# The latents' norm behind the experts: once per layer over all 512 tokens, or tile by tile beside the next tile's expert places

## What is computed

```python
def _rmsnorm(x, w):
    y = xf * lax.rsqrt(jnp.mean(xf * xf, axis=-1, keepdims=True) + EPS)
    return (y * w).astype(x.dtype)
for l in range(DEPTH):                       # DEPTH = 2
    h = _rmsnorm(x, norm1[l]) * (1 + sc1) + sh1
    x = x + g1 * _token_mixer(h, ...)[0]
    h = _rmsnorm(x, norm2[l]) * (1 + sc2) + sh2
    x = x + g2 * _peer(h, ...)               # 8 heads x 16 picked experts for each token
y = _rmsnorm(x, final_norm)
```

## Time and profile before

| | us |
|---|---|
| median of three runs | 4971.81 |
| the profiled execution | 4934.85 |
| its span in the trace | 4933.1 |
| PE busy | 3932.0 (80%) |
| DVE busy | 3078.9 (62%) |
| POOL busy | 2831.9 (57%) |
| ACT busy | 1199.2 (24%) |

### The profile page before, as it was taken

The page is one execution under the profiler, slowest core; times in us unless marked ns, Lnnn a source line. Parts: engine busy times, 40 slices in busy tenths (PEclk is TensorE's granted clock), DMA queues, the critical chain, the costliest instruction groups (busy, mean ns, idle before and its releaser), DMA issues.

```text
span 4933.1 us, 40947 instructions
## 1 busy us (share of the span) xinstructions
PE 3932.0 (80%) x11544; PEld 1863.3 (38%) x11544; DVE 3078.9 (62%) x6951; ACT 1199.2 (24%) x2524; POOL 2831.9 (57%) x2642
## 2 busy tenths in 40 slices
PE   5798889889777777788776787999787777777776
PEld 3674444334333333344342454444332222222222
DVE  8637898775556556555655777852557566566653
ACT  2433333211223222232111343231112111111111
POOL 0001556317677677777766444630767777777775
PEclk8798889999999999999999898999999999999999
DMA  8653889758999999999988766962889999999997
GB/s 306 230 180 144 295 312 389 272 199 318 345 365 358 356 379 379 379 400 400 380 327 336 254 230 238 369 242 79 313 333 379 367 384 383 370 398 383 389 392 299
DMA packets 425891, 1585.40 MB, mean 321 GB/s; under 512 B 47680, under 2 KB 55360, under 8 KB 408640
## 3 DMA queue, kind: packets, MB, share of 16 engines
q0 software_dynamic: 376800, 1394.77, 74.8%
q1 hardware_dynamic: 44256, 183.81, 10.0%
q10 hardware_dynamic: 4608, 4.20, 0.3%
HBM read 1577.87 MB, written 4.72 MB: 321 GB/s over the span
## 4 chain that ended last, share of the span: by engine, by line
PE 20%; DMA 18%; issue 5%; POOL 3%; DVE 2%; ACT 1%; DVEq 1%; ACTq 0%; POOLq 0%
PE pair L744 19%; DMA vbuf_lat<-in_expert_v,idx_lat 17%; POOL ubuf_lat L709 2%; POOL vbuf_lat L716 1%; DVE acc L1747 0%; PE pair L880 0%; PE pair L885 0%; DMA ubuf_ctx<-in_expert_u,idx_ctx 0%; DVE ubuf_ctx L1698 0%; DMA ubuf_lat<-in_expert_u,idx_lat 0%; ACT L1128 0%; DVEq L1569 0%; DVE hist_lat L1566 0%; DVEq L1741 0%; ACT on_lat L1128 0%
## 5 line engine op out<-in xcount | busy, mean ns | idle before, releaser
L744 PE MATMUL pair<-vbuf_lat,diag 128*128 128x512 f32 x4096 | 2036.2, 629 | 706.6 <-DMA vbuf_lat<-in_expert_v,idx_lat 674.6
L744 PEld LDWEIGHTS pair<-vbuf_lat,diag 128*128 128x128 f32 x4096 | 731.8, 195 | 1946.4 <-DMA vbuf_lat<-in_expert_v,idx_lat 1042.3
L716 POOL DMA_INDIRECT vbuf_lat<-in_expert_v,idx_lat x1024 | 1133.9, 1107 | 464.8 <-issue 220.1
L1698 DVE CUSTOM_DVE_ANT_0 ubuf_lat<-hT,ubuf_lat 128x1024 f32<-128x1024 f32 x768 | 936.1, 1224 | 702.2 <-DMA ubuf_lat<-in_expert_u,idx_lat 698.1
L709 POOL DMA_INDIRECT ubuf_lat<-in_expert_u,idx_lat x1024 | 1089.9, 1064 | 376.8 <-issue 226.2
L744 PE MATMUL pair<-hT,slot 128*128 128x512 f32 (+1 forms) x2048 | 578.3, 442 | 24.4 <-DVE hT L1428 15.9
L1128 ACT ACTIVATE diag<-cst,coef 128x128 f32<-128x128 f32 x1024 | 326.6, 390 | 1004.4 <-DVE coef L1704 1000.4
L709 POOL DMA_INDIRECT ubuf_ctx<-in_expert_u,idx_ctx x256 | 292.3, 1142 | 482.7 <-DVE araw L1698 307.3
L1698 DVE CUSTOM_DVE_ANT_0 ubuf_lat<-xnat,ubuf_lat 128x1024 f32<-128x1024 f32 x256 | 312.0, 1224 | 250.4 <-DMA ubuf_lat<-in_expert_u,idx_lat 248.3
L744 PEld LDWEIGHTS pair<-hT,slot 128*128 128x128 f32 x2048 | 319.2, 196 | 275.4 <-issue 262.4
L1128 ACT ACT_TABLE_LOAD x318 | 408.0, 1283 | 31.9 <-DVE mT_lat L1592 15.2
(11 more groups left out here) (313 smaller groups left out, 3148.7 us busy)
## 6 DMA issues: line engine op xcount, KB each, us to landing
slot<-in_w_query SPq DMA_DIRECT2D x32, 1024.0 KB, 5.6
modw<-in_w_mod_turned POOLq DMA_DIRECT2D x28, 1024.0 KB, 5.7
slot<-in_w_qk SPq DMA_DIRECT2D x16, 1024.0 KB, 6.8
slot<-in_w_v SPq DMA_DIRECT2D x16, 1024.0 KB, 5.9
slot<-in_w_r SPq DMA_DIRECT2D x16, 1024.0 KB, 7.9
wraw<-in_w_zg SPq DMA_DIRECT2D x32, 512.0 KB, 6.5
wraw<-in_w_zf SPq DMA_DIRECT2D x32, 512.0 KB, 6.5
wraw<-in_w_gla_out SPq DMA_DIRECT2D x32, 512.0 KB, 6.5
```

The source lines that it names most:

```text
L716: pool.indirect_dma_start(peer[s].v[n % ring_v][:, :], None, v_rows, bass.IndirectOffsetOnAxis(ap=index[:, p // PICKS, p % PICKS:p % PICKS ...
L744: return pe.matmul(out, lhsT, rhs, start=first, stop=last)
L1698: v.tensor_tensor_reduce(rows_of, x, rows_of, 1.0, 0.0, ALU.mult, ALU.add, araw[n % 3][:, p % GS:p % GS + 1]).then_inc(s_dot, 1)
```

## The change

The norm behind the experts is made per tile of 128 tokens. A new piece `tile_norms(l)` is woven into the experts of layer l on PE, ACT and DVE; its due times follow `updated_us(t)`, the time planned for the end of the tile's second update. It uses a 128 x 128 tile `tile_rs` and the columns 0 to 127 of `ps[1]`. The squares, the sum of squares, `rstd` and `norm` go out of the head of `mix(1, LAT)`, and `last_norm(LAT)` goes. The outputs are laid out in HBM by tile, and `y_sample` is stored in four pieces of one tile each, as each is normed.

```diff
+def updated_us(t):
+    return lat_place(PICKS * (t + 1) + 27) + 0.5 if t < TS // P - 1 else lat_added(TS // P * PICKS // GS) + 6.5
...
+            # PE
+            def tile_norms(l):
+                for t in range(NT[LAT]):
+                    yield updated_us(t) + 3.0
+                    n = l * NT[LAT] + t
+                    pe.wait_ge(s_tsq, n + 1)
+                    need(pe, s_trs, n)
+                    pe.wait_ge(s_xnc, l * (NT[0] + NT[1]) + NT[0] + NT[1])
+                    c0 = TP + t * P
+                    for k in range(KC):
+                        last = mm(ps[1][:, 0:P], ones[:, :], hT[:, k, c0:c0 + P], k == 0, k == KC - 1)
+                    last.then_inc(s_tss, 1)
...
+            # ACT
+            def tile_norms(l):
+                for t in range(NT[LAT]):
+                    n, c0 = l * NT[LAT] + t, TP + t * P
+                    yield updated_us(t) + 1.5
+                    act.wait_ge(s_xu[LAT], 2 * (n + 1))
+                    af(hT[:, :, c0:c0 + P], xT[:, :, c0:c0 + P], ACT.Square).then_inc(s_tsq, 1)
+                    yield updated_us(t) + 5.0
+                    act.wait_ge(s_tss, n + 1)
+                    need(act, s_th, n)
+                    af(tile_rs[:, :], ps[1][:, 0:P], ACT.Ln, bias=eps[:, :], scale=1.0 / D)
+                    act.drain()
+                    af(tile_rs[:, :], tile_rs[:, :], ACT.Exp, scale=-0.5).then_inc(s_trs, 1)
...
+            # DVE
+            def tile_norms(l):
+                for t in range(NT[LAT]):
+                    n, c0 = l * NT[LAT] + t, TP + t * P
+                    yield updated_us(t) + 8.0
+                    dve.wait_ge(s_trs, n + 1)
+                    h = hT[:, :, c0:c0 + P]
+                    spread = lambda column: column.to_broadcast([P, KC, P])
+                    tt(h, xT[:, :, c0:c0 + P], tile_rs[:, :].unsqueeze(1).to_broadcast([P, KC, P]), ALU.mult)
+                    dve.drain()
+                    if l == DEPTH - 1:
+                        tt(h, h, spread(cols0[:, 16:24].unsqueeze(2)), ALU.mult).then_inc(s_th, 1)
+                        continue
+                    tt(h, h, spread(nscale[l + 1][:, 0, :, LAT:LAT + 1]), ALU.mult)
+                    dve.drain()
+                    tt(h, h, spread(modT[l + 1][:, 0:KC, LAT:LAT + 1]), ALU.add).then_inc(s_th, 1)
...
             # SP
-            for k in range(0, KC, 2):
-                hold(sp, s_h[LAT], 2 * DEPTH * KC + k + 2)
-                sp.dma_start(y_sample[:, k:k + 2, :], hT[:, k:k + 2, COLS[LAT]]).then_inc(s_y, 16)
+            for t in range(NT[LAT]):
+                hold(sp, s_th, (DEPTH - 1) * NT[LAT] + t + 1)
+                sp.dma_start(y_sample[t], hT[:, :, TP + t * P:TP + (t + 1) * P]).then_inc(s_y, 16)
```

More of the change, by code:

```diff
@@ L453, in build @@
     assert e[0] <= end, (e[0], end)
+    tile_rs = place("tile_rs", [P, P], at=[area[CTX].end - P * 4])
     CONTEXT_BANK, CONTEXT_TURN = (0, 4), (0, 3)
@@ L536, in build @@
         s_x2 = [sem(f"x_done_of{s}") for s in range(2)]
+        s_tsq, s_tss, s_trs, s_th = sem("tile_squares"), sem("tile_square_sums"), sem("tile_rstd"), sem("tile_normed")
         s_zero = sem("zeros_set")
@@ L570, in z_no, with norm2_no @@
             return (2 * l + s) * KC + z
+        def norm2_no(l, s):
+            return 2 * l + 1 if s == CTX else l + 1
         def unit_no(l, s):
@@ L778, in mix @@
                     pe.wait_ge(s_sc, 2 * (2 * l) * PH)
-                sum_squares(s, 2 * l, b.ss)
+                by_tiles = s == LAT and l > 0
+                if not by_tiles:
+                    sum_squares(s, 2 * l, b.ss)
                 yield at(-9.0)
@@ L782, in mix @@
                 for k in range(KC):
-                    pe.wait_ge(s_h[s], (2 * l) * KC + k + 1)
+                    if by_tiles:
+                        pe.wait_ge(s_th, l * NT[LAT])
+                    else:
+                        pe.wait_ge(s_h[s], (2 * l) * KC + k + 1)
                     last = mm(b.lr, a.wlr[:, k, :], hs[k], k == 0, k == KC - 1)
@@ L958, in mix @@
                 pe.wait_ge(s_x1[s], l * KC + KC)
-                sum_squares(s, 2 * l + 1, b.ss)
+                sum_squares(s, norm2_no(l, s), b.ss)
             def loaded_qk(l, s, h):
@@ L1156, in mix @@
                     squares(s, None)
-                else:
+                elif s == CTX:
                     squares(s, (2, (l - 1) * KC))
@@ L1163, in mix @@
                     states(0)
-                rstd(s, 2 * l, b.ss)
+                if s == CTX or l == 0:
+                    rstd(s, 2 * l, b.ss)
                 yield at(-6.0)
@@ L1269, in mix @@
                 yield at(NORM2_US + 7.0)
-                rstd(s, 2 * l + 1, b.ss)
+                rstd(s, norm2_no(l, s), b.ss)
             def natural(l, s, t, source, dst):
@@ L1489, in mix @@
                 yield at(-28.0)
-                norm(s, 2 * l, lambda k: nscale[l][:, 0, k, s:s + 1], lambda k: modT[l][:, k, s:s + 1])
+                if s == CTX or l == 0:
+                    norm(s, 2 * l, lambda k: nscale[l][:, 0, k, s:s + 1], lambda k: modT[l][:, k, s:s + 1])
                 dve.wait_ge(s_tab, 16)
@@ L1598, in mix @@
                 yield at(NORM2_US + 9.0)
-                norm(s, 2 * l + 1, lambda k: nscale[l][:, 1, k, s:s + 1], lambda k: modT[l][:, 24 + k, s:s + 1])
+                norm(s, norm2_no(l, s), lambda k: nscale[l][:, 1, k, s:s + 1], lambda k: modT[l][:, 24 + k, s:s + 1])
             def choose(l, s, u, at):
```

27 lines of the change are left out of this document (12 added, 15 removed).

## The result

| | before | after |
|---|---|---|
| median of 20 runs each, same chip | 4962.37 us | 4973.95 us (4954.72 to 4983.75) |
| ratio | | 1.0024, 95% interval [1.0013, 1.0036]: +12 us [6, 18] |
| profiled execution, span | 4934.85, 4933.1 us | 4969.39, 4967.6 us |

The changed kernel is a little slower: the interval leaves "no change" out, but the difference is less than the 0.3% that the prediction had set as the least that can be told, and the time is inside the forecast range. The two profiled executions differ by 34.5 us. Part of that is chance: single executions of one kernel lie 30 to 50 us apart, and the profiled one of before was faster than all its runs here. I compare short stretches that begin at the same event, over as many traces as have them.

A forecast was written before the change was run, and what follows sets the result against it. Bound: the gather stream, tied to PE, in layer 1's experts; a chain over the norm before the mixer. Terms -10.1 - 9.8 + 11.1 + 8.7 + 2.0 = +1.9 us on median 4971.81: 4973.7, range 4960 to 4988 (4950 to 4992 with rivals).

The forecast's parts named there:

- The tail, -9.8: Behind layer 1's last tile: the shorter norm chain and last store end the span at 4923.3, 9.8 us earlier.
- sum to 4914.35: In layer 1's last tile norm: PE's sum of squares over 128 columns takes 1.95 us, ending at 4914.35.
- The mixer, -10.1: Between layer 0's experts and the next mixer: the norm per tile saves 10.1 us, bounds 7 to 18.5.
- PE resumes 10.1 us earlier: Into layer 1's mixer: PE could start 18.5 us earlier, but waits for DVE's key copy, which moves 10.1 us earlier.
- the shift stays: Behind the key copy: the mixer keeps its order and is PE-bound, so the 10.1 us gain lasts.
- Six mid-tile norms, +19.8: Tiles 0 to 2 of each layer: a 4.3 us stall each, costing 11.1 us in layer 1 and 8.7 in layer 0.
- the tiles are no longer than before: Sign of being wrong: the six gaps appear, yet the tiles do not lengthen (3 to 4 us each expected in layer 1).
- DVE's wait is covered: Mid-tile: dots come some 9 us late, hidden behind the held v gather; if not, 2 to 4 us more each.
- The rival with +7 for each norm there: Layer 0: DVE's backlog makes each of three norms cost about 2.9 + 7 us; sum +23, 4995; chance 0.18.
- The six stalls are swallowed: Rival, mid-tile: gathers in flight cover the 4.3 us waits, the six cost about 5; total -19, 4953; chance 0.22.
- The table switch: ACT between Ln and Exp: the switch costs 1.35 us as traced, not the skill's 2.66.
- Stores, +2.0: Three of four tile stores, now inside layer 1's experts, cost 2.0 us in all; 4.1 if transfer-bound, none if in gaps.

The follow-up runs named there:

- layer 1 only: Changed kernel with layer 0's tile norms taken out, its whole norm as in the kernel before; ratio to before 1.0002 [0.9979, 1.0024].
- layer 0 only: Changed kernel with layer 1's tile norms taken out, its norm and stores as in the kernel before; ratio to before 1.0036 [1.0018, 1.0054].
- ACT late: Changed kernel with ACT's Ln and Exp of the mid-layer tile norms put behind group 6's diagonals; ratio to before 1.0005 [0.9981, 1.0028].
- DVE late: Changed kernel with DVE's products of the mid-layer tile norms put behind group 7's mask and coefficients; ratio to before 1.0021 [1.0007, 1.0034].
- both late: Changed kernel with ACT's Ln and Exp behind group 6's diagonals and DVE's products behind group 7's coefficients; ratio to before 0.9985 [0.9961, 1.0009].

## Why the prediction came out as it did

The time was right within the bound: 4973.7 forecast, 4973.95 measured. That it agrees to 0.3 us is luck: it leans on a median of before that was 9 us higher (4971.81) than the one beside which after was timed. Against before, the sum said +1.9 and the two timings say +12 and +16. By its steps:

- **The tail, -9.8.** 18.5 us instead of 27.1 and 25.5: -7.0 to -8.6. The chain was right, and so were the in-order prices. The step "sum to 4914.35" was short: the sum took 3.57 and not 1.95, since PE had idled. So was the same step into the mixer (3.41), where 16.8 us were won at the first block and not 18.5. The store landed 3.5 us behind its issue. This term holds, 1 to 3 us too large.
- **The mixer, -10.1.** This is the step that failed: "PE resumes 10.1 us earlier", and "the shift stays". The wait for the key copy was foreseen. But the copy came only 4.9 us earlier: the gather that the norm had held came 7.9 earlier and not 10.1, and behind it DVE's dots now waited for their rows. The wait of 12.85 us that stood in front of the copy left PE at the lower clock, 6 us dearer over three products, a term that the prediction doesn't have. Net +0.7 in the two traces of after, against the three with the old order (both of before, layer 1 only). Over the six traces with that order (after twice, layer 0 only, ACT late, DVE late, both late) the mean is 760.2, -2.4 against 762.6. So 8 to 11 us of forecast gain were missing, about the whole of what the sum was off by. With the copy in the right place, and both norms' moves beside it, the gain came: -11.9. Even there 4 of 16 us were lost again, in a wait for DVE in the same head.
- **Six mid-tile norms, +19.8.** The mechanism was right and its chain is in the trace row by row (4.3 us late forecast; the earlier trace rows against PE's 3.28 us wait and POOL's 3.75). The gap of PE of 3 to 4 us is there at five of the six places of the first trace, at the sixth it is 1.50. Locally a place costs 4.5 us in layer 0 and 5.1 in layer 1 (15 places against 9 in each), 29 for six. At the end of the tiles less can be seen: +6.6 us (standard error 4.8) for the three of layer 0 and +11.7 (9.7) for those of layer 1, 18 in all. So the forecast is between what the places show and what the tiles show, and how much is given back behind the place can't be settled with tiles that vary so much. By this the prediction's own sign of being wrong ("the tiles are no longer than before") can't be read either. Sum by tiles: 18 + 0.7 - 7.8 = +11; by places: 29 + 0.7 - 7.8 = +22. The timings, +12 and +16, lie between.
- **DVE's wait is covered.** The text said so of layer 1 and doubted it for layer 0. In the kernel as it is, the waiting gather is one of v rows at all six places, so it is covered in both layers. In layer 1 moving DVE alone brought nothing, as forecast; that it was worth another 1.2 with ACT moved as well (31.2 to a mean of 30.0) is within the scatter. In layer 0 it is the wait that is left when ACT's is gone, in front of u rows. The rival with +7 for each norm there is too dear: a place in layer 0 costs no more than in layer 1, and layer 0's tiles grew by 2 us each, not by more than 5.
- **The six stalls are swallowed.** No: with both moved the places return to within 0.4 us of those without a norm in layer 0 and 1.2 in layer 1, and the timing of both late lies below that of after by more than the intervals ([-19, +4] against [6, 18]; some 7 us of this are the start). So the stalls were real and were paid, at least in part.
- **The table switch.** Ln ends at 4959.52, the load starts at 4959.57 and ends at 4960.85, Exp starts at 4960.86: 1.34 us, as the earlier trace rows had it. The Trainium skill (ScalarE: Activation LUTs, What ACT_TABLE_LOAD costs) would have 2.66; no row here shows the drain.
- **Stores, +2.0.** Nothing beyond chance was seen; the bound from the places, some 2 us for each, is too wide to tell 2.0 for all three from none.

## What to carry to other kernels

When a chain ahead of a queue gets shorter, follow the next operand of the queue to the instruction that makes it, and move that one too: here 17 us were won at the first block and 12 of them lost at the third, until one copy on DVE was given a better place, neither behind the dots nor so early that it held them. Work that is added to an engine which feeds a stream belongs behind the operand that the stream needs next, on every engine on which it waits: ACT's wait hid DVE's, removing DVE's alone showed little, and removing ACT's alone showed nothing in layer 0 and half of the cost in layer 1. And where single traces differ by 30 us, read a short stretch between two events that all kernels share, and count it over many tiles.

## What the runs showed of the hardware

- A wait of 12.85 us in which PE had nothing to do was followed by products at half rate (3.75 for 1.96, 3.78 for 1.98, granted clock 0.50), and by 16.54 for 14.08. With the key copy behind nine dots, one of 0.88 us was not, and one of 3.85 us later in that head was again (3.79 for 1.95). How long the low clock lasted didn't go by the length of the wait: 7.39 us before three slow products, 11.03 before one. Products without use in the wait kept the rate. Nobody need wait for them, and they returned 6 us.
- The same sum over 128 columns took 1.95 us in the stream and 3.41 or 3.57 at the two ends, where PE had stood (granted clock 1.00, 0.58 and 0.56): a short chain at the end of a stage is to be priced at the lower clock.
- A tile's store of 512 KB in pieces of 512 bytes landed 3.5 us behind its issue at the end of the span, in every kernel with one such store there. In the stream of gathers it took 3.5 to 5.5 us in after and 8.7 to 11.9 with both late. The context's store in such pieces took 15.6 before, 10.7 and 15.4 in the two traces of after, and 5.7 with DVE late: one such time is no measure of the next.
